# Two attentions: scaling the outputs of a pair of heads instead of the probabilities of each step

## What is computed

```python
s = jnp.einsum('bqkgd,bskd->bkgqs', q_blk, k_blk) * scale + bias
p = jax.nn.softmax(jnp.concatenate([s, sink_l], axis=-1), axis=-1)[..., :SPAN]
o = jnp.einsum('bkgqs,bskd->bqkgd', p, v_blk)
```

## Time and profile before

| | us |
|---|---|
| median of 3 runs | 1914.92 (1914.68 to 1914.97) |
| the profiled execution | 1917.37 |
| its span, first to last instruction | 1915.6 |
| PE busy in the span | 1897.8 |
| PE loading weights | 1567.2 |
| DVE busy | 964.2 |
| ACT busy | 772.1 |
| GpSimd busy | 182.8 |

### The profile page before, as it was taken

One profiled execution on the slowest core, in us unless ns is written; L12 is line 12 of the kernel. 1 busy time (PEld: TensorE's weight loads), 2 busy tenths in 40 slices (PEclk: granted clock), 3 DMA queues, 4 the chain that ended last, 5 costly groups with the idle time before them and its releaser, 6 DMA issues.

```text
span 1915.6 us, 25105 instructions
## 1 busy us (share of the span) xinstructions
PE 1897.8 (99%) x10458; PEld 1567.2 (82%) x10458; DVE 964.2 (50%) x1497; ACT 772.1 (40%) x1251; POOL 182.8 (10%) x196
## 2 busy tenths in 40 slices
PE   9999999999999999999999999999999999999998
PEld 7878888888888867888888888878887888888887
DVE  5693665553245284566553236443655555425523
ACT  5494433333333295433333334233764443212321
POOL 4112200000005031300000103000000020000000
PEclk9999999999999999999999999999999999999999
DMA  6512233334333311232233332331112323233222
GB/s 191 197 35 77 80 97 99 99 92 141 93 104 123 99 41 56 89 98 92 97 99 91 102 105 99 99 106 61 59 38 86 116 90 97 99 99 96 93 97 88
DMA packets 54136, 182.96 MB, mean 96 GB/s; under 512 B 6604, under 2 KB 10060, under 8 KB 53512
## 3 DMA queue, kind: packets, MB, share of 16 engines
q1 hardware_dynamic: 51528, 172.28, 28.2%
q0 software_dynamic: 2352, 9.02, 1.6%
q10 hardware_dynamic: 144, 0.06, 0.0%
HBM read 176.58 MB, written 4.76 MB: 95 GB/s over the span
## 4 chain that ended last, share of the span: by engine, by line
PE 88%; ACT 5%; DVE 5%; issue 1%; DMA 1%; SPq 0%; DVEq 0%; ACTq 0%
PE bank L1903 22%; PE bank L1904 22%; PE bank L1905 22%; PE bank L1922 2%; ACT prob_long L848 2%; PE bank L1923 2%; PE bank L1924 2%; ACT pt_short L837 1%; PE bank L2153 1%; PE bank L1683 1%; PE bank L1686 1%; PE bank L1691 1%; PE bank L1981 1%; PE bank L1982 1%; PE bank L1983 1%
## 5 line engine op out<-in xcount | busy, mean ns | idle before, releaser
L1155 DVE TENSOR_TENSOR w_lo<-w_raw,w_hi 128x1024 fp32r<-128x1024 f32 (+3 forms) x319 | 388.6, 1220 | 712.3 <-ACT w_hi L661 711.9
L661 ACT CAST w_hi<-w_raw 128x1024 fp32r<-128x1024 f32 (+3 forms) x319 | 322.0, 1010 | 555.0 <-DMA w_raw<-in_w_down 132.4
L1903 PE MATMUL bank<-h_hi,w_hi 128*128 128x512 f32 x1272 | 497.1, 391 | 0.8 <-DVE w_lo L1155 0.5
L1904 PE MATMUL bank<-h_lo,w_hi 128*128 128x512 f32 x1272 | 496.1, 390 | 0.0
L1905 PE MATMUL bank<-h_hi,w_lo 128*128 128x512 f32 x1272 | 495.9, 390 | 0.0
L1903 PEld LDWEIGHTS bank<-h_hi,w_hi 128*128 128x128 f32 x1272 | 239.5, 188 | 53.1 <-issue 2.2
L1905 PEld LDWEIGHTS bank<-h_hi,w_lo 128*128 128x128 f32 x1272 | 239.5, 188 | 50.2
L1904 PEld LDWEIGHTS bank<-h_lo,w_hi 128*128 128x128 f32 x1272 | 239.5, 188 | 49.5
L1903 PE MATMUL bank<-a_hi,w_hi 128*128 128x512 f32 (+1 forms) x676 | 261.5, 387 | 0.0
L1904 PE MATMUL bank<-a_lo,w_hi 128*128 128x512 f32 (+1 forms) x676 | 261.3, 387 | 0.0
L1905 PE MATMUL bank<-a_hi,w_lo 128*128 128x512 f32 (+1 forms) x676 | 261.3, 386 | 0.0
(11 more groups left out here) (328 smaller groups left out, 2551.6 us busy)
## 6 DMA issues: line engine op xcount, KB each, us to landing
w_raw<-in_w_gu SPq DMA_DIRECT2D x87, 512.0 KB, 3.5
w_raw<-in_w_mlp_in SPq DMA_DIRECT2D x32, 512.0 KB, 3.5
w_raw<-in_w_mlp_out SPq DMA_DIRECT2D x32, 512.0 KB, 3.6
w_raw<-in_w_down SPq DMA_DIRECT2D x32, 448.0 KB, 3.3
w_raw<-in_w_out SPq DMA_DIRECT2D x24, 512.0 KB, 3.6
w_raw<-in_w_down SPq DMA_DIRECT2D x16, 512.0 KB, 3.5
w_raw<-in_w_gates SPq DMA_DIRECT2D x16, 512.0 KB, 3.4
w_raw<-in_w_qk_b SPq DMA_DIRECT2D x14, 512.0 KB, 3.7
```

What stands on the lines that cost most here:

```text
L661: nc.scalar.copy(hi_of(v), raw_of(v)).then_inc(w_hi_done, 1)
L1155: nc.vector.tensor_tensor(lo_of(v), raw_of(v), hi_of(v).bitcast(F32), ALU.subtract).then_inc(w_split, 1)
L1903: mm(acc, w1, hi, start=start, stop=False)
L1904: mm(acc, w1, lo, start=False, stop=False)
```

## The change

In the two first attentions the probabilities stay as the exponentials left them, and PE turns them as soon as the exponentials are through. The row sums of a pair's eight rows of tiles (four steps, two heads) are kept, in `sums[..., of]`. After the last step of a pair DVE takes eight reciprocals at once, writes each 64 times in a row into `raw` (the spread roots), and PE turns these with the first step of the next pair (`turn`, second loop; behind the last pair there is one more turn for it alone). ACT copies them together with that step's turned probabilities into the upper half of the buffer in `pt_short`. `output_remainder` on DVE then multiplies the pair's product out of its bank by these, into `act_out`, rounds it to o_hi and takes the remainder o_lo. ACT no longer copies the output there. The third attention keeps its scalings. Left out below are declarations and counters.

```diff
...
@@ -445,6 +445,13 @@
         attention = [window_steps(), grid_steps(), dilated_steps()]
         pt_bufs = [pt_short, pt_short, pt_dil]
+        def turned_blocks(phase, d, steps):
+
+            begin, end = 0, 2 * len(steps[d].blocks) if d < len(steps) else 4
+            if phase < 2 and d and d % 4 == 0:
+                begin, end = 0 if d < len(steps) else 4, 8
+            return begin, end
+
         LAG_T, LAG_V, PROB_RING = (3, 3, 2), (4, 4, 3), (4, 4, 3)
         def prob_of(phase, s, half):
...
@@ -830,10 +837,12 @@
             def copy_turned(phase, d, steps):
                 if d >= 2:
                     act.wait_ge(pv_done, pv[0] + d - 1)
+                if phase < 2 and d % 4 == 2 and d > 2:
+                    act.wait_ge(o_scaled, scaled[0] + d // 4)
                 act.wait_ge(t_ready, turned[0] + 1)
-                n = 2 * len(steps[d].blocks)
-                dst = pt_of(phase, d)[:, :P * n].rearrange("p (n r q) -> p r n q", n=n, r=2)
-                src = turn_banks[:, :, :64 * n].rearrange("p r (n q) -> p r n q", n=n)
+                begin, end = turned_blocks(phase, d, steps)
+                dst = pt_of(phase, d)[:, P * begin:P * end].rearrange("p (n r q) -> p r n q", n=end - begin, r=2)
+                src = turn_banks[:, :, 64 * begin:64 * end].rearrange("p r (n q) -> p r n q", n=end - begin)
                 nc.scalar.activation(dst, src, ACT.Copy).then_inc(pt_copied, 1)
                 turned[0] += 1
@@ -845,17 +854,16 @@
                     for k, both in enumerate(st.pieces):
                         p = both[half]
                         part = prob_of(phase, s, half)[:, p["at"]:p["at"] + p["width"]]
+                        of = st.pair_no % 2 if phase < 2 else k
                         nc.scalar.activation(part, part, ACT.Exp, bias=top, scale=-1.0,
-                                             accum_out=sums[:, s % 4, half, k:k + 1]).then_inc(p_exp, 1)
+                                             accum_out=sums[:, s % 4, half, of:of + 1]).then_inc(p_exp, 1)
                 masked[0] += 2 * m
             def copy_output(phase, d, steps, o_hi):
                 if not steps[d].last:
                     return
                 act.wait_ge(pv_done, pv[0] + d + 1)
-                dst, src = o_hi[:, steps[d].pair, :], bank_in(phase, 6 + steps[d].pair_no % 2)[:, :]
-                if phase == 2:
-                    dst, src = unclassed(dst, src)
+                dst, src = unclassed(o_hi[:, steps[d].pair, :], bank_in(phase, 6 + steps[d].pair_no % 2)[:, :])
                 nc.scalar.copy(dst, src).then_inc(o_hi_done, 1)
             def softmax(phase, o_hi, beside=None, last_values=None, read=None):
@@ -867,12 +875,10 @@
                     if s == 2 and last_values:
                         values_by_tile(last_values, *read)
                     if phase < 2:
-                        if 0 <= s - LAG_T[phase] < n:
+                        if 0 <= s - LAG_T[phase] <= n:
                             copy_turned(phase, s - LAG_T[phase], steps)
                         if s < n:
                             exps(phase, s, steps[s])
-                        if 0 <= s - LAG_V[phase] < n:
-                            copy_output(phase, s - LAG_V[phase], steps, o_hi)
                         if last_values and s >= n:
                             hi_to(last_values[1] + 2 + min(s - n, 2))
                     else:
...
@@ -1282,12 +1290,21 @@
                         return
                     st = steps[d]
                     o_count[0] += 1
+                    acc = bank_in(phase, 6 + st.pair_no % 2)[:, :]
+                    if phase < 2:
+                        dve.wait_ge(pt_copied, turned[0] + d + 2)
+                        dve.wait_ge(pv_done, pv[0] + d + 1)
+                        o = act_out[:, st.pair_no % 2, :]
+                        nc.vector.tensor_tensor(o, acc, pt_of(phase, d + 1)[:, 4 * P:8 * P], ALU.mult).then_inc(o_scaled, 1)
+                        dve.wait_ge(o_scaled, o_count[0])
+                        nc.vector.tensor_copy(o_hi[:, st.pair, :], o).then_inc(o_hi_done, 1)
+                        dve.wait_ge(o_hi_done, o_count[0])
+                        nc.vector.tensor_tensor(o_lo[:, st.pair, :], o, o_hi[:, st.pair, :].bitcast(F32),
+                                                ALU.subtract).then_inc(o_ready, 1)
+                        return
                     dve.wait_ge(o_hi_done, o_count[0])
-                    dst, src = o_lo[:, st.pair, :], bank_in(phase, 6 + st.pair_no % 2)[:, :]
-                    lead = o_hi[:, st.pair, :].bitcast(F32)
-                    if phase == 2:
-                        lead = unclassed(lead, src)[0]
-                        dst, src = unclassed(dst, src)
+                    lead = unclassed(o_hi[:, st.pair, :].bitcast(F32), acc)[0]
+                    dst, src = unclassed(o_lo[:, st.pair, :], acc)
                     nc.vector.tensor_tensor(dst, src, lead, ALU.subtract).then_inc(o_ready, 1)
                 for s in range(n + LAG_V[phase]):
@@ -1320,21 +1337,23 @@
                                 masked[0] += 1
                     d = s - 1
                     if 0 <= d < n:
-                        m, i = len(steps[d].pieces), d % 4
-                        expd[0] += 2 * m
-                        dve.wait_ge(p_exp, expd[0])
-                        total = sums[:, i, :, 0]
-                        if m > 1:
-                            nc.vector.tensor_reduce(den[:, i, :], sums[:, i, :, :m], axis=AX.X, op=ALU.add).then_inc(den_done, 1)
-                            dens[0] += 1
-                            dve.wait_ge(den_done, dens[0])
-                            total = den[:, i, :]
-                        nc.vector.reciprocal(rden[:, i, :], total).then_inc(rden_done, 1)
-                        rdens[0] += 1
-                        dve.wait_ge(rden_done, rdens[0])
-                        for half in range(2):
-                            part = prob_of(phase, d, half)[:, :steps[d].width]
-                            nc.vector.tensor_scalar(part, part, rden[:, i, half:half + 1], None, ALU.mult).then_inc(p_ready, 1)
+                        expd[0] += 2
+                        if phase < 2 and steps[d].last:
+                            dve.wait_ge(p_exp, expd[0])
+                            of = steps[d].pair_no % 2
+                            nc.vector.reciprocal(rden[:, :, :], sums[:, :, :, of]).then_inc(rden_done, 1)
+                            rdens[0] += 1
+                            dve.wait_ge(rden_done, rdens[0])
+                            spread = rden[:, :, :].rearrange("p i (h o) -> p (i h) o", o=1).to_broadcast([P, 8, HD])
+                            nc.vector.tensor_copy(raw[:, of, :].rearrange("p (n d) -> p n d", n=8), spread).then_inc(roots_spread, 1)
+                        elif phase == 2:
+                            dve.wait_ge(p_exp, expd[0])
+                            nc.vector.reciprocal(rden[:, d % 4, :], sums[:, d % 4, :, 0]).then_inc(rden_done, 1)
+                            rdens[0] += 1
+                            dve.wait_ge(rden_done, rdens[0])
+                            for half in range(2):
+                                part = prob_of(phase, d, half)[:, :steps[d].width]
+                                nc.vector.tensor_scalar(part, part, rden[:, d % 4, half:half + 1], None, ALU.mult).then_inc(p_ready, 1)
                     if phase < 2:
                         output_remainder(s - LAG_V[phase] - 1)
                         if last_values and s >= n:
...
@@ -2059,14 +2079,14 @@
                 if d == 0:
                     wait_reads((act_read, 0, 0))
-                if not 0 <= d < len(steps):
+                if not (0 <= d < len(steps) or phase < 2 and d == len(steps)):
                     return
-                blocks = steps[d].blocks
                 if turned[0]:
                     pe.wait_ge(pt_copied, turned[0])
-                for half in range(2):
+                for half in range(2 if d < len(steps) else 0):
+                    blocks = steps[d].blocks
                     ready[0] += 1
-                    pe.wait_ge(p_ready, ready[0])
+                    pe.wait_ge(p_exp if phase < 2 else p_ready, ready[0])
                     first_key = steps[d].pieces[0][half]["first_key"]
                     for kt, (first, w) in enumerate(blocks):
                         keys = slice(first_key + first, first_key + first + w)
@@ -2075,12 +2095,21 @@
                             last = nc.tensor.transpose(ps[4 + part][:w, at_:at_ + 64],
                                                        prob_of(phase, d, half)[rows(part), keys],
                                                        ident[rows(part), 64 * part:64 * part + 64])
+                if phase < 2 and d and d % 4 == 0:
+                    pe.wait_ge(roots_spread, heads[0] + d // 4)
+                    for i in range(4):
```

(41 more changed lines are left out.)

## The result

The changed kernel takes **1927.37 us** (median of four runs, 1924.88 to 1928.01), the kernel before on the same chip 1914.80: ratio 1.0065, 95% interval 1.0048 to 1.0082. It is 12.6 us slower; 1924.7 was forecast. A second series gave 1926.57 against 1915.47, ratio 1.0058 (1.0044 to 1.0071), 11.1 us.

A forecast was written before the change was run, and what follows sets the result against it. The prediction took ACT to bound the windowed attention and DVE the grid one. Windowed +4.2 and grid +5.6 gave +9.8 us, from the median 1914.92 to 1924.7 us; whole range 1917.5 to 1931.

The forecast's parts named there:

- the transposes behind the end: End of each of the first two attentions: the last eight transposes lie on PE's path, +0.4 us each.
- some tenths: Grid attention, first pair: relief from its contended scalings, named only in the rival that the change is faster, chance 0.03.
- DVE costs 2.2 today: Grid attention, six periods: DVE's scalings cost 2.2 of 39.48 us beyond ACT's own work; removing them gives this back.
- the lump: DVE, first two attentions: reciprocal, spread, scaling, rounding, remainder in one piece ahead of the next masks, 2.32 us.
- Windowed, +3.8 in six periods: Windowed attention: ACT's waits for masks, 4 x 0.64 + 0.49 + 0.95, less 0.2 of ACT work: +3.8 us.
- Grid, +3.8 and 1.4 for GpSimd: Grid attention: -2.2 - 0.2 + 6.2 = +3.8 us, plus 1.4 for copies slowed by GpSimd's additions in two pairs.
- only when exps(s-1) are through: DVE, first two attentions: what its output work waits for before it begins, behind masks(s); no size of its own.
- while ACT waits, PE gains that room: First two attentions: ACT's waits of 0.5 to 1.1 us a pair give PE room for its added transposes.
- The 0.7: Grid attention: remainder slowed by GpSimd for its two SBUF inputs, 2 x 0.35 = 0.7 us, not in the sum.
- Lump hidden: Rival, first two attentions: DVE's piece is short enough that ACT finds its masks ready, 1913.1 us fully hidden; chance 0.16.
- PE as a second bound: Rival, first two attentions: transposes and ACT's waits add instead of overlapping, 5.0 us more, 1929.7; chance 0.09.

The follow-up runs named there:

- e6: Kernel before the change, biases left out and GpSimd's mask additions cut to one column each: 1912.40 us, ratio 0.9988 to before.
- e7: Changed kernel with the same work, its DVE output work in four pieces behind four different masks: 1915.29 us, ratio 1.0006 to before.
- e2: Changed kernel with rounding and remainder of a pair's output moved one step later, behind the next masks: 1917.52 us, ratio 1.0012 to before.
- e4: Changed kernel with the eight transposes of a pair's reciprocals done twice, to the same place: 1929.11 us, ratio 1.0076 to before.
- e1: Changed kernel again, unaltered, as measure on the same chip: 1926.57 us, ratio 1.0058 to before.
- e3: Changed kernel with the copy that spreads the reciprocals done twice: 1933.44 us, ratio 1.0092 to before.
- e5: Changed kernel, biases left out and GpSimd's mask additions in the grid attention cut to one column each: 1924.03 us, ratio 1.0051 to before.
- e8: DVE output work in four pieces in the grid attention alone, windowed attention as before the change: 1913.48 us, ratio 0.9992 to before.
- e9: Second series of the kernel with four pieces in the grid attention alone: 1913.72 us, ratio 0.9995 to before.

## Why the prediction came out

The time came out inside the forecast's own range, and the mechanism is the one forecast. That the parts add up so closely is some luck. In the profiles the windowed attention costs 4.8 us (4.2 forecast) and the grid 5.8 (5.6 forecast), but the grid's figure hides errors that cancel: its six periods cost 1.0 more than forecast, the transposes behind the end little (0.2 to the table load, where 0.4 stood), and up to the first wide copy the changed kernel is 0.7 faster (13.83 us from the first exponential, against 14.53 to the same step's copy before), since the first pair's scalings beside GpSimd are gone (e6, without the additions, takes 13.82). The forecast had these "some tenths" in a rival and not in its sum.

- **What bounds the kernel.** Right: the time moved in the two attentions, 10.5 of 10.8 us, by waits of ACT. "DVE costs 2.2 today" in the grid is right as a number (2.4 in e6), but the scalings as such are not the reason: without GpSimd's additions they stay, and periods fall to 6.10 to 6.32 us, ACT's own work (24.56 / 4 = 6.14, in the memory heads 12.76 / 2 = 6.38). They are on the path only where the additions slow them, in the periods of 6.80, 7.17 and 6.76 us, and the chain of the earlier trace rows lies in these. With the lump cut up (e7) six periods fall by 1.3 us and not 2.4, since PE sets them then.
- **The lump.** Right: 2.32 us forecast, 2.37 found; spreading copy and rounding took 0.43, 0.42 was taken. By the table of the Trainium skill's "VectorE: DVE Perf Modes" (errata section) a copy would have been 0.33 and the lump 0.18 shorter. But the same section says that this row of the table gives too short a time for a single operation, and has a measured fixed term of about 150 cycles in place of the 58; by that the estimate is 0.42. The trace agrees with it: 0.43.
- **Windowed, +3.8 in six periods.** Found 4.2: waits of 0.59, 0.61, 0.61 where 0.64 stood, 0.47 and 0.49 where 0.64 and 0.49 stood, and 0.88 where 0.95 stood. By these figures the waits are 0.35 below the forecast, but the brackets count from the end of the instruction before, and the forecast counted in slots, which end some 0.1 us sooner (a copy of 768 columns is busy 0.82 us in a slot of 0.71). In slots the wait at 114.12 is 0.71: the periods grew by 0.71, 0.69, 0.70, 0.70, 0.38 and 0.98 us, where 0.61 four times, 0.46 and 0.92 stood. e2 shows the mechanism.
- **Grid, +3.8 and 1.4 for GpSimd.** Found 6.2, where 5.2 stood. An uncontended period of 7.20 us is ACT's own work plus the wait of 1.07 as forecast (24.56 / 4 + 1.07 - 0.03 = 7.18), but it has a second way to come about: in slots ACT waits 0.12 for the scaled output (its copy at 712.75 starts 0.08 us behind the scaling's end, as that at 704.92 does) and then 1.00 for the mask (0.89 in the brackets); and the lump begins when masks(s) are through, which wait for PE's scores, and not "only when exps(s-1) are through". In the pair of the row at 710.80 both arrive together: the reciprocal starts at 711.40, right behind the mask and 0.13 us behind ACT's next instruction, where 0.14 stood. That PE's way is a bound there is what e4 shows. The forecast left it out, and "while ACT waits, PE gains that room" is true in four windowed periods and false in the grid (e4).
- **GpSimd.** The mis-sized term: two lumps grew by 8.28 + 8.24 - 2 x 7.20 = 2.1 us, 1.4 was charged. The copies grew by 0.2 to 0.45, where 0.35 was taken, and the remainder, not charged, from 0.69 to 1.10 (the rows at 112.92 and 705.56). "GPSIMD Engine Reference", section 1, of the Trainium skill named just this case, two inputs from SBUF; the trace agrees, and the scaling with one input from PSUM kept its 0.68. The 0.7 that the prediction left out for it belonged in. e6 adds that the additions cost the kernel before at least as much, so none of it is seen as a net loss of the change.
- **The rivals.** "Lump hidden" was priced at 1913.1 without PE: e7, which hides it, gives 1915.29, since PE's transposes set the windowed pairs then. "PE as a second bound": not in four windowed pairs; in the last two and in the grid PE stands in the loop beside the lump (e4), and behind the lump it sets both attentions (e7).

## What to carry to other kernels

Less work on an engine that waits its turn in a loop can cost time, if what is left comes in one piece: compare the longest piece in front of what the next engine needs with the time until that engine asks for it, not the sums. Put such work in pieces of which each fits that slack (here 1.7 and 1.25 us); the same instructions were 10 to 11 us faster so. Before pricing a relief, look which engine is second: behind ACT's 7.18 us a pair stood PE with some 7.15 (e2's 7.4 less 0.25), and the eight added transposes went straight onto it.

## What was not expected of the hardware

The same program can run a stretch of an attention at the lower of TensorE's two clock levels in one execution and not in another. In the second profile of the changed kernel (e1) PE waited for the contended lump (the one beside GpSimd's additions), and then worked at the lower level:
```profile
696.00:700.00 4.00, 2.56 (x30) 1.47 (x28) 3.77 (x14) 2.32 (x7) 2.41 (x4) 1.00 0.01 3
700.00:710.00 10.00, 10.00 (x84) 6.90 (x84) 5.39 (x19) 6.77 (x21) 9.01 (x14) 0.50 0.10 29
```
PE is busy 2.56 of 4.00 us, then the granted clock is 0.50 (1.2 GHz) for ten, and 84 matmuls take all of them. In the same ten us of the first profile it did 112 in 8.14 us:
```profile
696.00:700.00 4.00, 2.99 (x36) 1.79 (x32) 3.77 (x13) 2.02 (x8) 2.93 (x4) 1.00 0.02 4
700.00:710.00 10.00, 8.14 (x112) 5.46 (x112) 6.61 (x25) 8.05 (x26) 8.77 (x14) 1.00 0.09 29
```
There PE had been busy 2.99 of the 4.00, and the clock stayed, as it did in e4's grid. The pair took 10.26 us instead of 8.24, and the stretch from the first grid exponential to the table load 149.99 instead of 147.63, 2.4 more. e3, whose lump is longer, had the same between 714 and 722 us (0.50). It would be natural to put the lower clock down to the waits for the contended lump, and e5, e7 and e8, without them, had it nowhere in the grid. But e9, the same kernel as e8, had it too, in its first grid pair, ahead of the first output. These are e9 and then e8:
```profile
680.00:684.00 4.00, 2.90 (x38) 1.98 (x36) 1.98 (x12) 3.82 (x14) 2.13 (x4) 0.98 0.61 187
684.00:687.40 3.40, 3.40 (x32) 2.49 (x28) 1.50 (x7) 2.20 (x9) 2.70 (x5) 0.53 0.03 11
...
680.00:684.00 4.00, 2.90 (x37) 2.05 (x36) 1.98 (x12) 3.78 (x12) 1.68 (x4) 1.00 0.55 159
684.00:687.40 3.40, 3.40 (x48) 2.69 (x48) 2.10 (x10) 3.40 (x12) 3.24 (x6) 1.00 0.16 49
```
PE was busy 2.90 of 4.00 us in both, and then did 32 matmuls in one and 48 in the other; up to the first wide copy e9 took 1.6 us longer. And e2 and e4, with contended waits, kept the clock in the grid. So what decides the fall is open: the waits may make it likelier, and they are not needed for it. The changed kernel's timed runs would fit a fall in some of them (1924.88 at a mean clock of 0.999, 1926.83 to 1928.01 at 0.996 to 0.997), but where their lower clock fell no trace shows. It may be the 0.3 to 1.8 us by which the differences of the medians exceed the profiled one of 10.8.
